# First weights between the halves of X, rests of the first splits shared by two engines, recurrent mixer by halves of heads

## The reference, cut to what matters

```python
def first_block(x, ...):
    for layer in range(2):
        h = rms_norm(x, norm_mix_g[layer])
        x = x + (mixer_ab(h, ...) if layer == 0 else mixer_rglru(h, ...))
        h = rms_norm(x, norm_ffn_g[layer])
        x = x + hierarchical_moe(h, ...)
    return rms_norm(x, norm_final_g)

def mixer_ab(h, w_in, a_ln_g, a_ws, a_ws_b, b_conv_w, w_out):
    u, v, gate_b, gate_c, xb = jnp.split(h @ w_in, ..., axis=-1)      # five pieces of 512 columns
    u, v = gelu(u), layer_norm(gelu(v), a_ln_g)
    ws = jnp.where(causal, a_ws, 0.0)                                 # 4 heads, 128 x 128
    y_a = u * (einsum('hts,bcshd->bcthd', ws, v in chunks) + a_ws_b)
    y_b = gate_b * causal_conv(gate_c * xb, b_conv_w)
    return concatenate([y_a, y_b]) @ w_out

def mixer_rglru(h, w_in, conv_w, conv_b, w_a, b_a, w_x, b_x, lam, w_out):
    gate, xr = jnp.split(h @ w_in, [1024], axis=-1)
    gate = gelu(gate)
    xr = causal_conv(xr, conv_w) + conv_b                             # 4 taps
    r = sigmoid(xr_head @ w_a + b_a)                                  # 8 heads of 128
    i = sigmoid(xr_head @ w_x + b_x)
    log_a = 8 * r * log_sigmoid(lam)
    a, b = exp(log_a), sqrt(-expm1(2 * log_a)) * (i * xr)
    hseq = scan(h_t = a_t * h_(t-1) + b_t)                            # over the 512 positions
    return (gate * hseq) @ w_out
```

## Time and profile before

| | us |
|---|---|
| median of 3 runs | 2706.59 |
| lowest, highest | 2702.04, 2707.36 |
| the profiled execution, as timed | 2703.67 |
| its span in the profile | 2702.3 |
| TensorE busy | 2592.2 (96%) |
| VectorE busy | 1148.7 (43%) |
| ScalarE busy | 899.4 (33%) |
| GpSimd busy | 360.3 (13%) |

### The profile page before, as it was taken

How to read it: one execution, slowest core, us unless ns; L and a number is a source line. 1 busy time by engine, 2 the same in 40 slices (tenths; PEclk the granted TensorE clock), 3 DMA queues, 4 the chain that set the end, 5 groups by cost and what they waited for, 6 DMA issues and landing times.

```text
span 2702.3 us, 33251 instructions
## 1 busy us (share of the span) xinstructions
PE 2592.2 (96%) x13432; PEld 1818.3 (67%) x13432; DVE 1148.7 (43%) x2169; ACT 899.4 (33%) x1740; POOL 360.3 (13%) x165
## 2 busy tenths in 40 slices
PE   7998999999998899999979999999999999999999
PEld 6875444444766444444467778888888777888887
DVE  2543323332646332232256343562554534365254
ACT  3431111111464111111154554442345445443233
POOL 3200000000331000000021011222222001122222
PEclk9999999999898999999989999999999999999999
DMA  5229999999311999999932011223231201223212
GB/s 198 79 81 418 419 422 421 421 421 418 118 62 57 419 419 421 421 421 420 421 122 79 32 63 48 94 94 110 68 113 59 79 33 62 79 94 109 78 63 86
DMA packets 139003, 543.28 MB, mean 201 GB/s; under 512 B 18784, under 2 KB 30304, under 8 KB 89696
## 3 DMA queue, kind: packets, MB, share of 16 engines
q1 hardware_dynamic: 129232, 536.94, 50.8%
q10 hardware_dynamic: 9616, 4.18, 0.6%
HBM read 538.99 MB, written 2.10 MB: 200 GB/s over the span
## 4 chain that ended last, share of the span: by engine, by line
PE 90%; DVE 5%; ACT 2%; issue 2%; DMA 0%; POOL 0%; SPq 0%; DVEq 0%; ACTq 0%
PE ps L603 23%; PE ps L1363 16%; PE ps L605 14%; PE ps L1385 8%; PE ps L1338 5%; PE ps L625 4%; PE ps L537 4%; PE ps L1398 3%; PE ps L1939 2%; PE ps L1399 2%; PE ps L1912 2%; PE ps L1931 1%; PE ps L538 1%; PE ps L455 1%; DVE w L278 1%
## 5 line engine op out<-in xcount | busy, mean ns | idle before, releaser
L603 PE MATMUL ps<-w,w 128*128 128x512 f32 x2976 | 679.9, 390 | 2.6 <-POOL w L278 2.6
L603 PEld LDWEIGHTS ps<-w,w 128*128 128x128 f32 x2976 | 559.0, 188 | 119.7 <-POOL w L278 3.4
L278 POOL TENSOR_TENSOR w<-w,w 128x1024 fp32r<-128x1024 f32 (+2 forms) x139 | 337.2, 2435 | 2182.9 <-ACT w L270 2182.9
L1363 PE MATMUL ps<-w,w 128*64 128x512 f32 x2048 | 451.6, 594 | 1.8 <-issue 1.8
L605 PE MATMUL ps<-w,w 128*128 128x512 f32 (+1 forms) x1872 | 410.9, 381 | 18.2 <-issue 15.2
L270 ACT ACTIVATE w<-w 128x1024 fp32r<-128x1024 f32 (+2 forms) x260 | 252.7, 1001 | 436.2 <-PE ps L603 196.9
L605 PEld LDWEIGHTS ps<-w,w 128*128 128x128 f32 x1872 | 339.9, 189 | 85.5 <-issue 19.7
L278 DVE TENSOR_TENSOR w<-w,w 128x1024 fp32r<-128x1024 f32 (+2 forms) x121 | 200.7, 1666 | 386.8 <-ACT w L270 384.4
L1363 PEld LDWEIGHTS ps<-w,w 128*64 128x64 f32 x2048 | 146.0, 137 | 285.6 <-issue 285.6
L1615 DVE TENSOR_TENSOR X<-ps,X 128x512 f32<-128x512 f32 x256 | 163.0, 682 | 163.0 <-PE ps L1399 161.9
L1385 PE MATMUL ps<-w,w 128*64 128x512 f32 x1024 | 226.8, 595 | 0.8 <-ACT w L1449 0.8
(11 more groups left out here) (251 smaller groups left out, 2325.3 us busy)
## 6 DMA issues: line engine op xcount, KB each, us to landing
w<-in_moe_w_gate SPq DMA_DIRECT2D x128, 1024.0 KB, 14.0
w<-in_moe_w_up SPq DMA_DIRECT2D x128, 1024.0 KB, 16.4
w<-in_moe_w_down SPq DMA_DIRECT2D x128, 1024.0 KB, 13.0
w<-in_w_up SPq DMA_DIRECT2D x40, 1024.0 KB, 5.1
w<-in_w_down SPq DMA_DIRECT2D x20, 1024.0 KB, 5.1
w<-in_w_in SPq DMA_DIRECT2D x16, 1024.0 KB, 5.1
w<-in_ab_w_in SPq DMA_DIRECT2D x10, 1024.0 KB, 5.1
w<-in_c_w_in SPq DMA_DIRECT2D x8, 1024.0 KB, 5.1
```

The lines of the kernel that those rows point to most:

```text
L278: up(self.wlo[self.low[s][0]], lane.e.tensor_tensor(lo, raw, hi.bitcast(F32), ALU.subtract))
L603: ins = pe.matmul(bank[:, :], wp[:, k, P * o:P * o + P], ap(k0 + k), start=first, stop=stop)
L1363: ins = pe.matmul(bank[64 * e:64 * e + 64, :], XG[p % 3][:, 4 * u + k, 64 * e:64 * e + 64], w[e][:, k, :], start=(u == 0 and k == 0), stop ...
```

## The change

At the start: SyncE issues the first unit of weights between X's second and third piece. WS and lnB are issued by ScalarE only behind the first six splits, and GpSimd masks WS behind its first rests. `ring_start` begins at -6, so that rests 0, 2 and 4 are VectorE's, and 1, 3 and 5 GpSimd's.

In the recurrent mixer: the sixteen gate matmuls become two groups of eight, heads 0 to 3 ahead of gt 0 and heads 4 to 7 ahead of gt 1. The weights `w_a`, `w_x` come in two units of 512 KB. ScalarE, VectorE and GpSimd do sigmoids, exp, square, tanh, roots, scans by these halves; the squares of heads 0 to 3 go to the place of the gate (GT[0]), which the gelu of gt 0 then waits for. The splits of halves 12 and 13 (gt 1's first unit, whose slot the first gates' unit frees) are made behind the first four heads' work.

```diff
-        self.n_loaded = self.n_dense = self.n_expert = self.limit = self.ring_start = 0
+        self.n_loaded = self.n_dense = self.n_expert = self.limit = 0
+        self.ring_start = -NSPLIT
...
         for c in range(NT):
+            if c == 2:
+                W.load_up_to(1)
             sp.dma_start(X[:, c, :], A["x"][0, P * c:P * c + P]).then_inc(s_x[c], 16)
...
-            act.dma_start(WS[:, :, :], A["a_ws"][0].rearrange("h t s -> t h s")).then_inc(s_ws, 16)
-            act.dma_start(lnB, A["a_ln_g"][0].partition_broadcast(P)).then_inc(s_ws, 16)
             def x_there(c):
...
             scalar_first_halves(0, 3, SPLITS)
+            act.dma_start(WS[:, :, :], A["a_ws"][0].rearrange("h t s -> t h s")).then_inc(s_ws, 16)
+            act.dma_start(lnB, A["a_ln_g"][0].partition_broadcast(P)).then_inc(s_ws, 16)
...
             vector_norm(apply, ((0, 2),))
+            W.lo(0, V)
             vector_half(rows, 0)
             vector_norm(apply, ((2, 1), (3, 1)))
+            W.lo(2, V)
             vector_half(rows, 1)
+            W.lo(4, V)
...
         def gpsimd():
+            low_first_halves(0, G)
             G.wait_dma(s_ws, 32)
...
-            low_first_halves(0, G)
...
-            for key in (("xr", 1), ("gt", 0)):
-                tensor_product(key, ALL4, 512, H, ba, feature=True)
...
+            tensor_product(("xr", 1), ALL4, 512, H, ba, feature=True)
+            for s in range(2):
+                gates = W.of["gates"][s]
+                wg = W.need_raw(gates, PE)[:, 0:1024].rearrange("p (g h j) -> p g h j", g=2, h=4)
+                for h in HEADS[s]:
+                    PE.wait_ge(x_conv, h + 1)
+                    for g in range(2):
+                        bank = banks.take(ba)
+                        n = up(ba.full, pe.matmul(bank[:, :], wg[:, g, h % 4, :], XC[:, h, :], start=True, stop=True))
+                W.raw_consumed_at[gates.n] = (ba.full, n)
+                tensor_product(("gt", s), ALL4, 512, H, ba, feature=True)
...
+            decays(HEADS[0])
+            for h in behind_gates:
+                W.hi(h)
+            scalar_product(("gt", 0), gelu_0, second=lambda: roots(HEADS[0]))
+            decays(HEADS[1])
+            roots(HEADS[1])
...
-                if h == 5:
-                    for m in range(4):
-                        low(m)
+            factors(HEADS[0])
+            for h in behind_gates:
+                W.lo(h, V)
+            vector_product(("gt", 0), second=lambda: scans(HEADS[0]))
+            factors(HEADS[1])
+            scans(HEADS[1])
+            for m in range(4):
+                low(m)
...
+            inputs(HEADS[0])
+            for h in behind_gates:
+                W.lo(h, G)
+            gpsimd_product(("gt", 0))
+            inputs(HEADS[1])
```

More of the change, by code:

```diff
@@ L996, in plan_lru @@
         w = A["c_w_in"][0]
[L997 to L1001, removed]
+        for s in range(2):
+            plan_cols(("xr", s), w, 1024 + 512 * s, 512)
+        for s in range(2):
+            W.add("gates", [(4, 128, A[name][0][4 * s:4 * s + 4].rearrange("h i j -> i h j")) for name in ("c_w_a", "c_w_x")],
+                  split=False)
+            plan_cols(("gt", s), w, 512 * s, 512)
         plan_out("lruo", A["c_w_out"][0])
@@ L1012, in mixer_rglru, with squared @@
         YL = at(20480, 8, 512, dt=F32R)
-        gates = W.of["gates"][0]
         H = rows.H
+        HEADS = (range(0, 4), range(4, 8))
+        behind_gates = late_halves(("xr", 1), 2)
+        def squared(h):
+            return GT[0][:, h, :] if h < 4 else XT[:, h - 4, :]
         def tensor():
             tensor_first_product(rows, ("xr", 0), 4, 512, ba, True)
-            for key in (("xr", 1), ("gt", 0)):
-                tensor_product(key, ALL4, 512, H, ba, feature=True)
[L1020 to L1028, removed]
+            tensor_product(("xr", 1), ALL4, 512, H, ba, feature=True)
+            for s in range(2):
+                gates = W.of["gates"][s]
[7 more added lines that the diff above has]
+                tensor_product(("gt", s), ALL4, 512, H, ba, feature=True)
             tensor_out("lruo", (lambda k: YH[:, k, :], lambda k: YL[:, k, :]), lambda k: PE.wait_ge(ylo, k),
@@ new lines, in roots, with gelu_0 @@
+            def roots(hs):
+                for h in hs:
+                    S.wait_ge(q_done, h + 1)
+                    up(b_root, act.activation(RB[:, h, :], RB[:, h, :], ACT.Sqrt))
+            def gelu_0():
+                for o in range(4):
+                    bank = ba.next(S)
+                    S.wait_ge(q_done, 1 + o)
+                    bank_to(GT[0][:, o, :], bank[:, :], ACT.Gelu_apprx_tanh)
+            decays(HEADS[0])
+            for h in behind_gates:
+                W.hi(h)
@@ L1101, in taps, with factors, scans @@
                         up(x_conv, ins)
[L1102 to L1106, removed]
+                vector_product(("xr", s), taps, tail=2 * s)
+            def factors(hs):
+                for h in hs:
+                    V.wait_ge(a_sq, h + 1)
+                    up(q_done, dve.scalar_tensor_tensor(RB[:, h, :], squared(h), 1.0, RB[:, h, :], ALU.add, ALU.mult))
+            def scans(hs):
+                for h in hs:
+                    V.wait_ge(b_root, h + 1)
+                    V.wait_ge(i_x, h + 1)
+                    vstep(dve.tensor_tensor(IB[:, h, :], IB[:, h, :], RB[:, h, :], ALU.mult))
+                    up(scanned, dve.tensor_tensor_scan(RB[:, h, :], AA[:, h, :], IB[:, h, :], 0.0, ALU.mult, ALU.add))
             def low(m):
@@ L1129, in gpsimd, with inputs @@
             gpsimd_late(late)
[L1130 to L1134 removed]
+            for s in range(2):
+                gpsimd_product(("xr", s), tail=2 * s)
+            def inputs(hs):
+                for h in hs:
+                    G.wait_ge(ba.free, 8 + 4 * (h // 4) + 2 * h + 2)
+                    up(i_x, pool.tensor_tensor(IB[:, h, :], IB[:, h, :], XC[:, h, :], ALU.mult))
+            inputs(HEADS[0])
[3 more added lines that the diff above has]
+            inputs(HEADS[1])
             for m in range(4):
[L1136 removed]
+                G.wait_ge(ba.free, 8 + 8 + m + 1)
                 G.wait_ge(scanned, m + 1)
```

45 lines of the change are left out of this document (15 added, 30 removed).

## The result

The changed kernel takes 2683.71 us in the median of four runs (2682.82 to 2688.58), the kernel before 2706.07 in the median of its four (2702.04 to 2707.36): ratio 0.9924, 95% interval 0.9906 to 0.9941. The prediction was 2683, faster, and its range 2676 to 2690. Its two terms, -4.4 us at the start and -17.9 in the recurrent mixer, came out at -5.2 and -17.8. But the profiled execution gained only 15.3 us in its span: 0.6 us went between the two places that the change touches, and 7.1 of the remaining 22.4 behind the second.

A forecast was written before the change was run, and what follows sets the result against it. TensorE was taken as the bound (90% of the chain), so only its idle or slow-clock time could pay. Start -4.4 and mixer -17.9 gave -22.3 us: 2681.4 from the profiled execution, 2684.3 from the median; 2683 was taken, range 2676 to 2690.

The forecast's parts named there:

- When the unit lands: Start: the first unit of weights lands at 11.2 us, where it landed at 15.86.
- When products begin: Start: TensorE goes from its last transpose into products at 15.05 us instead of 19.43, a gain of 4.4 us.
- The rest of half 1 does not hold: Start: GpSimd ends this rest at 19.3 us, ahead of TensorE's need at about 20.5.
- The same clock shape: Start: TensorE's clock rises as before, so the gain is 4.4 us, between bounds of 3.1 and 5.8.
- The 6.92 us that only shift: Start, 27.85 to 34.77 us: the same chain in the same order, moved earlier as a block.
- upper bound of 5.8: Start: largest gain in us, if the clock rises early and the 48 matmuls end at 22.0 us.
- rival 2: Start: first unit stays near 15 us, only the faster rest's 1.1 us remains; gain 19.0, about 2686 us; chance 0.07.
- Scans end: Recurrent mixer: VectorE's scans end at 805.4 us, the last one delayed by GpSimd's rest of 19.
- Hold of 0.3 to 0.4 us: Recurrent mixer, ahead of the output product: TensorE waits this long instead of 15.19 us, a gain of 17.9 us.
- Table loads: Recurrent mixer, ScalarE: each load costs 1.28 us without the skill's 1.38 us drain, which would leave about -15.
- The carry: Behind both places: TensorE's chain and the experts' transfers begin earlier by what the mixer gains; sum -22.3 us.
- the span behind the mixer is unchanged in length: Behind the mixer: a sign that would show the forecast, with everything after taking as long as before.

The follow-up runs named there:

- after_again: The changed kernel itself, unaltered, run once more beside the other runs of its call; 2682.74 us (2682.45 to 2689.0).
- s_rests: The kernel before with only rests 0, 2 and 4 given to VectorE, the queues' order left as it was; 2705.5 us, ratio 1.000.
- late4: The changed kernel with four repeated scans of head 7 on VectorE ahead of the low parts of heads 0 to 3; 2697.15 us, one run.
- low_early: The kernel before with the recurrent heads' first four low parts issued behind each scan instead of all behind the sixth; 2706.17 us, ratio 1.0007.
- again: The changed kernel itself, unaltered, run and profiled a second time; 2685.63 us (2682.28 to 2689.06).

## Why the prediction was right

**The start.** *When the unit lands:* 11.2 predicted; ScalarE's copy of it starts at 11.15. *When products begin:* 15.05 predicted, 14.74 measured; the last transposes (to 15.09) overlap. *The rest of half 1 does not hold:* wrong. It ended at 17.06 + 2.39 = 19.45, near the predicted 19.3, but the first 24 matmuls took 4.00 us and not the 5.4 of the lower clock, so TensorE was there 0.77 us earlier than the rest. *The same clock shape:* wrong, in favour of the change: the second 24 took 3.15, and 48 took 22.65 - 14.74 = 7.91 with the wait in it, against 8.42. *The 6.92 us that only shift:* 29.57 - 22.65 = 6.92. Sum 4.69 + 0.51 = 5.20 in place of 4.4, inside the bounds. In after_again the start gave 6.72 us (50.92 - 44.20), more than the upper bound of 5.8: there the clock stayed up behind the wait for rest 3, which the bound took as unchanged.

What the working passed over: the hold ahead of 34.77 is named in it, but not what it costs, 2.3 us of waiting and in most profiles some clock. It carried the 6.92 us as a block, rightly, but one moved line there gave 2.4 to 3.8 us more at the first product, where the reordered queues gave 5.1. And rival 2 gave VectorE's share 1.1 us with the old order; s_rests gives it 0.4.

**The mixer.** ScalarE's and VectorE's rows in the changed kernel's timeline, with 4.59 us to be added for the clock of the prediction:

```profile
770.62 2.64 ACT L681 ACTIVATE w<-ps 128x512 f32<-128x512 f32 x4 [0.50 <-PE ps L604]
...
775.52 4.73 ACT L681 ACTIVATE w<-ps,PK 128x512 f32<-128x512 f32 x8
780.27 1.28 ACT L1064 ACT_TABLE_LOAD   x1
781.56 0.72 ACT L1064 ACTIVATE w<-w,SM 128x512 f32<-128x512 f32 x1
...
790.55 2.19 ACT L1074 ACTIVATE w<-w 128x512 f32<-128x512 f32 x4
```
```profile
796.77 0.67 DVE L1138 TENSOR_TENSOR w<-w,w 128x512 f32<-128x512 f32 x1
797.47 3.30 DVE L1139 TENSOR_TENSOR_SCAN w<-w,w 128x512 f32<-128x512 f32 x1
800.69 2.47 DVE L1143 TENSOR_TENSOR w<-w,w 128x512 fp32r<-128x512 f32 x4
```

- Gelus end: 777.9 predicted, 773.26 + 4.59 = 777.85 measured. Second sigmoids end: 785.2 and 784.84.
- Scans end: 805.4 predicted, 800.77 + 4.59 = 805.36. The last scan met GpSimd's rest (796.81, 2.88 us) and took 3.30 instead of 1.22, ending 1.08 us behind that pass: the term of the sum for it, "when that pass did plus its own length", held.
- Hold of 0.3 to 0.4 us: 0.20. Output product at full clock: 22.04 against 21.8. Gain 22.41 - 4.59 = 17.82, predicted 17.9.
- Table loads: the load ends at 781.55 and exp starts at 781.56. Two loads lie between the last sigmoid and the first root; with a drain of 1.38 us at each, as the Trainium skill ("ScalarE: Activation LUTs", section "What ACT_TABLE_LOAD costs") has it, the rests would by an estimate have come 2.8 us later. By late4 nearly all of that would have been waiting. The trace of the changed kernel doesn't agree with the rule: exp follows its load by 0.01 us, and the first root (790.55) follows the load at 789.26, of 1.28, by 0.01 too. The term without it stands.

**The carry.** "Both begin earlier by what the mixer gains" failed first at the routers. The chain of waits at the first and the second router, before and then in the changed kernel's first profile:

```profile
196.51 1.96 PE ps L1306 x16
875.96 1.96 PE ps L1306 x16
```
```profile
191.33 3.38 PE ps L1346 x16
853.55 3.36 PE ps L1346 x16
```

The granted clock is 1.00 in the second of these rows and 0.57 in the last two. The first router is slow in seven of the fourteen profiles, one with the old mixer (low_early) among them, and at 1.96 in again and after_again. The second starts 22.41 us earlier than before and ends 21.0 earlier. It took 3.36 to 3.62 us in all seven profiles with the new mixer in which TensorE doesn't wait ahead of the output product, and 1.96 in all seven in which it does: the six with the old mixer, and late4. That the two hang together is shown; why isn't. Behind it the shift was 19.06 at attention 1 and 15.4 from there to the end in the first profile, 18.8 at the end in again and 21.4 in after_again. So the step "the span behind the mixer is unchanged in length" failed in all three profiles, by 7.1, 4.6 and 3.6 us: 22.41 - 15.3, 23.4 - 18.8 and 25.0 - 21.4.

**Why the total came out all the same.** The start gave 0.8 us more than the sum; falls of the clock in later stages took back 3.6 to 7.1. That the median of four runs came out at 2683.71, 0.7 us from the 2683, is in part luck. Side by side the gains were 22.4, 18.1 and 22.6 us against the predicted 22.3, and over all 14 executions of the changed kernel (2684.4) and all 59 of the kernel before (2705.06) it is 20.7. The mechanism at both places was right; the carry behind them was off by about as much as the scatter. None of the rivals happened: the hold was 0.2 us; the unit came early; ScalarE's banks were empty ahead of the second gates; VectorE and GpSimd met, at 768.59 and 774.36 (scans of 3.31 and 3.35) as well as at 797.47, but the first two lay under gt 0 and the gates.

## What to carry to other kernels

Cost a hold at its waiting time and, as a range, the clock behind it (here 2.30 + 0 to 1.74, 7.33 + 1.62 and 15.19 + 3.10), and before speeding up a step ask what hides it: a rest twice as fast was worth nothing with the new order of the queues, while a copy moved in front of eight others took away 2.4 to 3.8 us. Look inside blocks that "only shift" for such a wait. And when a gain is of the size of the scatter (here 1.5 to 4.6 us of median from 5 us in the trace), judge it by its place in the trace; the median of five runs can't.

## What the runs showed of the hardware

One kernel's executions differ by up to 7 us of 2684, and the longer ones have the lower mean granted clock (0.986 to 0.989): the same part of attention ran at 0.51 in one and at 1.00 in another. So the gain of a profile can be 7 us off the one at the edited place; that an edit moves where the clock falls far behind it isn't shown, since the same kernel does this unaltered.

At the start the clock came up sooner when products followed the transposes directly: 24 matmuls took 3.11 to 4.25 us and the next 24 3.13 to 3.15, while in the old order, where TensorE stood still for about 4 us first (4.40 in the earlier trace rows), 48 took 7.32 to 8.67.

Behind one and the same wait of 2.3 us the clock was at its lower level at first in seven profiles (0.61 in again, 24 matmuls from 29.6 to 34 us) and stayed at 1.00 in three (after_again, 37 matmuls from 29.5 to 34). Within either order of the queues the three that stayed up are those whose matmuls ahead of the wait had been the fastest: 24 in 3.11 and 3.35 us against 3.61 to 4.00, and 48 in 7.68 against 8.32 to 8.67. Ten profiles show this; its reason isn't shown.
